# Expert inputs gathered from whole float32 rows, four one-time weight places, and transpositions moved between matrix products

## What is computed

```python
# t: 256 tokens x 1024; each token chooses 2 of the 8 experts of one group
combine = einsum('nk,nke->ne', top_w, one_hot(eid, 32))
for e in range(32):
    h = silu(t @ w_exp_gate[e]) * (t @ w_exp_up[e])
    y = y + combine[:, e:e + 1] * (h @ w_exp_down[e])
```

## Time and profile before

| | before |
|---|---|
| median of 3 runs | 1607.51 us (1607.12 to 1608.62) |
| the profiled execution's own time | 1607.49 us |
| its span | 1605.7 us |
| TensorE products busy | 1496.4 us (93%) |
| VectorE, ScalarE, GpSimd busy | 713.0, 574.6, 419.0 us |
| HBM read | 378.95 MB, mean 237 GB/s |
| mean granted TensorE clock | 0.984 of full speed |

### The profile page before, as it was taken

How to read it: one execution, slowest core, us unless ns; L and a number is a source line. 1 busy time by engine, 2 the same in 40 slices (tenths; PEclk the granted TensorE clock), 3 DMA queues, 4 the chain that set the end, 5 groups by cost and what they waited for, 6 DMA issues and landing times.

```text
span 1605.7 us, 23320 instructions
## 1 busy us (share of the span) xinstructions
PE 1496.4 (93%) x9442; PEld 1032.5 (64%) x9442; DVE 713.0 (44%) x1294; ACT 574.6 (36%) x779; POOL 419.0 (26%) x316
## 2 busy tenths in 40 slices
PE   5899999999999899999999998799989799999996
PEld 2788888888667444443344343477878678878785
DVE  2678887666436812111111121428222634334672
ACT  2432325554433322222121121344344355364662
POOL 0000000011000110000000000259867685757553
PEclk9999999999999999999999999999989899999998
DMA  8632225435778899999999999566436343434331
GB/s 310 204 127 96 79 79 173 139 107 165 265 264 295 360 378 420 421 422 422 422 422 422 422 422 422 204 231 210 132 130 222 110 166 106 158 111 151 106 134 64
DMA packets 120877, 381.10 MB, mean 237 GB/s; under 512 B 9302, under 2 KB 11134, under 8 KB 96222
## 3 DMA queue, kind: packets, MB, share of 16 engines
q1 hardware_dynamic: 120798, 380.02, 63.0%
HBM read 378.95 MB, written 1.05 MB: 237 GB/s over the span
## 4 chain that ended last, share of the span: by engine, by line
PE 67%; DMA 19%; DVE 4%; POOL 3%; ACT 3%; issue 2%; SPq 1%; POOLq 0%; DVEq 0%; ACTq 0%
DMA arena<-in_w_exp_up 17%; PE ps L786 12%; PE ps L793 12%; PE ps L787 12%; PE ps L1207 7%; POOL w_lo L2432 3%; PE ps L968 3%; PE ps L967 3%; PE ps L974 3%; PE ps L1219 2%; PE ps L867 2%; PE ps L887 1%; PE ps L1361 1%; ACT w_hi L2514 1%; PE ps L1230 1%
## 5 line engine op out<-in xcount | busy, mean ns | idle before, releaser
L2432 POOL TENSOR_TENSOR w_lo<-ring,w_hi 128x512 fp32r<-128x512 f32 x280 | 378.0, 1385 | 135.0 <-ACT w_hi L2514 123.3
L2514 ACT ACTIVATE w_hi<-ring 128x2048 fp32r<-128x2048 f32 x130 | 246.9, 1912 | 318.0 <-PE ps L793 148.6
L786 PE MATMUL ps<-w_hi,xt_hi 128*128 128x512 f32 x512 | 201.8, 394 | 0.2 <-ACT w_hi L2514 0.2
L787 PE MATMUL ps<-w_hi,xt_lo 128*128 128x512 f32 x480 | 187.0, 390 | 0.0
L1538 DVE TENSOR_TENSOR w_lo<-ring,w_hi 128x2048 fp32r<-128x2048 f32 x60 | 137.1, 2286 | 89.8 <-ACT w_hi L2514 89.4
L786 PE MATMUL ps<-w_hi,yt_hi 128*128 128x512 f32 x352 | 140.4, 399 | 5.5 <-DVE yt_lo L1531 2.7
L793 PE MATMUL ps<-w_lo,xt_hi 128*128 128x512 f32 x512 | 127.3, 391 | 5.1 <-POOL w_lo L2432 5.1
L1207 PE MATMUL ps<-arena 128*32 128x512 f32 x1056 | 118.9, 593 | 11.0 <-DMA arena<-in_w_exp_up 11.0
L2092 DVE TENSOR_SCALAR selT<-ps 128x256 fp32r<-128x256 f32 x32 | 13.6, 424 | 248.2 <-ACT arena L2845 248.2
L1207 PE MATMUL ps<-ring,arena 128*32 128x512 f32 x992 | 111.7, 593 | 12.0 <-DMA ring<-in_w_exp_up 11.0
L2432 POOL TENSOR_TENSOR w_lo<-ring,w_hi_ahead 128x512 fp32r<-128x512 f32 x8 | 9.9, 1271 | 422.6 <-ACT w_hi_ahead L2833 421.2
(11 more groups left out here) (323 smaller groups left out, 2378.1 us busy)
## 6 DMA issues: line engine op xcount, KB each, us to landing
ring<-in_w_in SPq DMA_DIRECT2D x40, 1024.0 KB, 5.1
ring<-in_b_w_in SPq DMA_DIRECT2D x40, 1024.0 KB, 5.1
arena<-in_w_exp_gate SPq DMA_DIRECT2D x33, 1024.0 KB, 23.0
arena<-in_w_exp_up SPq DMA_DIRECT2D x33, 1024.0 KB, 25.0
arena<-in_w_exp_down SPq DMA_DIRECT2D x32, 1024.0 KB, 23.3
ring<-in_w_exp_down SPq DMA_DIRECT2D x32, 1024.0 KB, 23.3
ring<-in_w_exp_gate SPq DMA_DIRECT2D x31, 1024.0 KB, 23.1
ring<-in_w_exp_up SPq DMA_DIRECT2D x31, 1024.0 KB, 25.0
```

Of the source, the lines that this page charges most:

```text
L786: pe.matmul(o[:, tt, :], hi[:, k, x_], w[:, c, :], start=(bias is None and j == 0 and c == 0), stop=False)
L787: pe.matmul(o[:, tt, :], lo[:, k, x_], w[:, c, :], start=False, stop=False)
L2432: ins = pool.tensor_tensor(w_lo2[:, slots_of[n], k, :], ring[:, slots_of[n], k, :], w[:, k, :].bitcast(F32), ALU.subtract)
L2514: act.activation(part_of(n)[1][:, :, :], ring[:, slots_of[n]], ACT.Copy).then_inc(S("w_hi_full"), 1)
```

## The change

- The bf16 parts go. `h_moe` is written to another place and stays as whole float32 rows, `sel` is float32, and `gather` does 2 products for a chunk, 16 for a pair. ScalarE's and VectorE's splitting instructions and the waits on `h_left` go.
- `extra` has four places (`EXTRA = 4`). The last two are filled after both router products (`routed`). The slots of expert 0's first four units are refilled with expert 4's units at once. The gains of the second norm are loaded after the third pair.
- Odd expert units 0, 1, 2 are asked for at `tail` 1,0, 1,1 and 2,0, units 4 and 5 at `tail` 6,0.
- `yT` is turned between tiles 9, 10, 11 and the first output units, `oT`'s first piece before the last value product, without `stay_busy`; ScalarE's and VectorE's shares move with them. The remainder of the first half of `bT` goes ahead of the second half's `normed_product`.

```diff
@@ places and order of SyncE
-        sel = nc.alloc_sbuf_tensor_at("sel", [P, NT, P], BF16, offset=ARENA_AT + 4 * (free0 + 4096))
+        sel, _ = carve(NT, P, on=free0 + 4096)
-        extra = [carve(UC, W, on=on)[0] for on in (o_S, o_S + 2048)]
+        extra = [carve(UC, W, on=on)[0] for on in (o_S + 2048, o_S, o_XT2, o_XT + 2048)]
-        h_parts = [nc.alloc_sbuf_tensor_at("h_part%d" % i, [P, NT, D], BF16, offset=ARENA_AT + 4 * (free0 + 1024 * i)) for i in range(3)]
-        h_rest, _ = carve(NT, D, on=o_XT + 2048)
-        h_moe, _ = carve(NT, D, on=o_qT)
+        h_moe, _ = carve(NT, D, on=free0)
...
-                if n in (at_unit["tail", 6, 0], at_unit["tail", 6, 1], at_unit["tail", 7, 0]):
-
-                    sp.wait_ge(S("unit_done"), end_of("ret", 1, 4))
-                    expert_unit(0, 1, n - at_unit["tail", 6, 0], 0)
-                if n == at_unit["tail", 7, 0]:
+                ahead = [at_unit["tail", 1, 0], at_unit["tail", 1, 1], at_unit["tail", 2, 0]]
+                if n in ahead:
+
+                    sp.wait_ge(S("retT_turned"), 4)
+                    expert_unit(0, 1, ahead.index(n), 0)
+                if n == at_unit["tail", 6, 0]:
...
+                sp.wait_ge(S("routed"), NT)
+                extra_unit(2)
+                extra_unit(3)
+                for k in range(6):
+                    sp.wait_ge(S("unit_done"), n_before + k + 1)
+                    expert_unit(4 if k < EXTRA else 2, 0, k, 0)
...
@@ TensorE
-                    for i, part in enumerate(h_parts):
-                        for tt in range(NT):
-                            mm = pe.matmul(ps[:, 0 if half else 2, o_:o_ + P], part[:, tt, P * k:P * (k + 1)], sel[:, tt, :],
-                                           start=(i == 0 and tt == 0), stop=(i == 2 and tt == NT - 1))
+                    for tt in range(NT):
+                        mm = pe.matmul(ps[:, 0 if half else 2, o_:o_ + P], h_moe[:, tt, P * k:P * (k + 1)], sel[:, tt, :],
+                                       start=(tt == 0), stop=(tt == NT - 1))
...
+            gemm_parts("a", 8, ("a", 8), xt2_hi, xt2_lo)
+            for t in range(9, 12):
+                gemm_parts("a", t, ("a", t), xt2_hi, xt2_lo)
+                turn_y(t - 9)
+            for j in range(4):
+                pair_evacuated(pe, ("yT", j))
+                gemm_unit("a_out", 0, j, yt_hi, yt_lo, 4)
+                if j == 0:
+                    turn_y(3)
+            gemm_parts("a_out", 1, ("a_out", 1), yt_hi, yt_lo, nk=4, half="y_half")
...
+                        if (g, c) == (2, 3):
+                            turn_output(0)
...
-                if c == 0:
-                    stay_busy(claim(("oT", c)), 12)
@@ VectorE
-            h_first_rest(0)
...
-            h_first_rest(1)
-            h_second_rest(0)
-            h_second_rest(1)
...
+                if t:
+                    rest_part("yT", t - 1, yt_hi, yt_lo)
+            rest_part("yT", 3, yt_hi, yt_lo)
...
                 product_scale(tt, 1, 4)
+                if tt:
+                    rest_tokens("bT", 0)
...
-            rest_tokens("bT", 0)
...
+                        if c == 3:
+                            rest_part("oT", 0, ot_hi, ot_lo)
                         join_last(c)
+                        if c == 2:
+                            gate_output(0)
...
-                if BKIND[t] == "z":
-                    gate_output(BIDX[t])
-            for c in range(2):
-                rest_part("oT", c, ot_hi, ot_lo)
+                if t == 19:
+                    gate_output(1)
+            rest_part("oT", 1, ot_hi, ot_lo)
@@ ScalarE
-            h_lead(0)
...
-            for tt in range(NT):
-                act.wait_ge(S("h_left"), tt + 1)
-                act.activation(h_parts[1][:, tt, :], h_rest[:, tt, :], ACT.Copy).then_inc(S("h_part"), 1)
...
-            for c in range(4):
-                lead_part("yT", c, yt_hi)
+                if t >= 9:
+                    lead_part("yT", t - 9, yt_hi)
+            lead_part("yT", 3, yt_hi)
...
-            leading_to(first["b_out"])
```

More of the change, by code:

```diff
@@ L53 @@
 PER_ROUND = 6 * NE
+EXTRA = 4
 RING2 = 4
@@ L260, in build @@
             slots_of.append(n % RING2 if n < n_before else expert_slot((n - n_before) // 6 % 2, (n - n_before) % 6) if n < first["a"] else (n - first["a"]) % RING2)
-            fills.append(slots_of.count(slots_of[n]))
+            fills.append(slots_of.count(slots_of[n]) - (n >= first["a"] and slots_of[n] in EVEN_SLOTS[:EXTRA]))
         fills_before = [slots_of[:n_before].count(k) for k in range(ALL_SLOTS)]
@@ L560, in weights @@
         def weights(odd, k, second=False):
-            if second and not odd and k < 2:
+            if second and not odd and k < EXTRA:
                 return extra[k]
@@ L1188, in arrived @@
                 s_ = expert_slot(odd, k)
-                if order == "second" and not odd and k < 2:
-                    pe.wait_ge(S("extra_full%d" % k), 16)
+                if order == "second" and not odd and k < EXTRA:
+                    pe.wait_ge(S("extra_full%d" % (k // 2)), 32)
                 else:
-                    missed = s_ in EVEN_SLOTS[:2] and order != "first"
+                    missed = s_ in EVEN_SLOTS[:EXTRA] and order != "first" and not (rd and s_ < RING2)
                     pe.wait_ge(full_of(s_, rd), e * 8 + 16 * (filled_times(s_, rd) + 1 - missed))
@@ L2228, in _ @@
                 dve.tensor_tensor(v, v, a_u[:, :, W * t:W * (t + 1)], ALU.mult).then_inc(S("y_gated"), 1)
-            for c in range(4):
-                rest_part("yT", c, yt_hi, yt_lo)
+                if t:
+                    rest_part("yT", t - 1, yt_hi, yt_lo)
+            rest_part("yT", 3, yt_hi, yt_lo)
             def part_sums(i, done):
```

44 lines of the change are left out of this document (12 added, 32 removed).

## The result

The changed kernel takes 1594.93 us (median of seven runs, 1589.88 to 1599.87); the kernel before, run beside it, 1608.62 us. The ratio is 0.9911 with a 95% interval of 0.9891 to 0.9931. The profiled execution is the one of 1594.93 us; its span is 1593.1 us, 12.6 us under the span of the kernel before (1605.7).

A forecast was written before the change was run, and what follows sets the result against it. Transfers were taken to bound the experts from 686 us, TensorE the rest, with three holes behind the experts. Gains of 7.5 (experts together) + 9.6 + 4.0 + 5.3 = 26.4 us gave 1581.1 us, range 1574 to 1591.

The forecast's parts named there:

- Part 1: Expert weight stream: two more one-time places leave two units less to carry after the stream resumes, 5.0 us gained.
- Part 2: First refills of expert slots: issued sooner, stream resumes 1.7 us earlier; 0.8 us more from a deeper queue.
- Part 3: Experts' input: float32 gather without split copies; first gate product 0.8 us earlier, pair about 1.0 us shorter but hidden.
- no saving: Rival on the experts' gather: 16 products take 3.5 us, pair 28.1 us, start 1.3 us later; 1582.5 us, 5%.
- The rival in which TensorE becomes the bound of all the experts: Expert loop: slow float32 gather makes a pair 31.6 us, total 1631 us; 4%.
- Part 4: Retention output stage: three early expert units delay its weights, TensorE 2.7 us later (0 to 7.5).
- Parts 5 to 7: Behind the experts: earlier yT turnings, bT remainder and oT turning gain 9.6, 4.0 and 5.3 us.
- No GpSimd remainder ends last: Rival on yT and oT: GpSimd's weight remainders end last, half of 14.9 us is lost; 1588.5 us, 9%.
- Prefetch dear, nothing earlier: Rival on early units: they cost 7.5 us, stream resumes no sooner; 1586 us, or 1590 with holes partly closed; 12%.

The follow-up runs named there:

- 3: The changed kernel with two one-time places instead of four, all else alike; 1593.49 us, ratio 0.9909.
- 1: The kernel before with only the moved yT and oT turnings and the earlier bT remainder; 1591.74 us, ratio 0.9888.
- 5: The kernel before with the moved turnings, earlier bT remainder and four one-time places, keeping its bfloat16 gather and its issue points for early expert units; 1587.71 us.
- kernel 2: The changed kernel with the five early expert units put back to where the kernel before issues them; 1588.09 us, ratio 0.9877.
- 10: The kernel before with only the yT turnings moved between the product tiles; 1599.90 us, ratio 0.9934.
- 11: The kernel before with only the earlier bT remainder and the moved oT turnings; 1599.93 us, ratio 0.9937.
- 6: As kernel 2, but three expert units issued earlier, in stretches where its transfers are idle; 1588.33 us, ratio 0.9868.
- second execution: The changed kernel measured once more with no edit; 1593.41 us, ratio 0.9898.
- kernel 7: As kernel 2, but the first early expert unit again issued ahead of the retention output stage's units; 1592.7 us.
- 8: As kernel 2, but the four one-time places hold units of expert 4 instead of expert 2, third pair written out ahead of the loops; 1591.43 us.

## Why the prediction went wrong, and where it was right

The spans differ by 12.6 us: 2.4 us lost ahead of 418 us, where the kernels are alike and 1.6 us are the clock's fall at 404 us; 6.6 lost in the stage; 0.7 between the stage and the first gate product; 2.7 gained in the experts; 19.7 gained behind them.

- *Part 1, two more places: 5.0 us forecast, about 0.5 measured (3).* This is the step that failed most. The working took the units in place as subtracted from a stream that then never stops. But the stream's lead over TensorE is bounded by the number of places, and a one-time place is one that does not come back: what it holds more at 555 us is missed in the hole at 596 us. The prediction looked for the hole ahead of the first refill only. With the bfloat16 gather, 1 and 5 differ by parts 1 and 2 together, and by 2.1 us in the experts, which is still far from the forecast.
- *Part 2, earlier resumption: 1.7 and 0.8 us forecast.* The first refill is indeed issued 3.66 us after the first gate product (568.79 for 565.13) and not 7.1; and in kernel 2, whose start is that of before, the window of 556 to 564 us has 401 GB/s where the earlier trace rows have 36. In after the start is so late that the places are full again: 176 GB/s from 564 to 572 us. Both together gave 1.5 us in the experts: 461.4 us is the mean of the four kernels with two places and the bfloat16 gather (before, 1, 10, 11), 459.9 that of the five with four places and the float32 gather. From the first gate product on, the sum had some 9.4 us.
- *Part 3, the gather: mis-sized by two.* The count behind the earlier trace rows was of instructions, not of products; the rows' x16 are eight products. At 256 columns 3.45 us for 8 are 0.43 us each, four cycles of 2.4 GHz for a column; at 128 columns it is a little more (0.24 us), and the Trainium skill (FP8 and Floating Point Precision, TensorE Precision Notes) was right with its four passes where the prediction said that the trace disagreed. The start of the experts is 0.7 us later instead of 0.8 earlier (103.3 us from the stage to it in before and 1, 104.0 in after, 2 and 6, all without a fall of the clock at 510 us). Between before and 2, the first gather and what follows up to the gate product take 4.97 us for 4.01, and TensorE's wait ahead of the second router product is 1.11 us for 1.56, so the forecast's 0.5 us for the copies was right and its 0.3 us for the gather was a loss of 1.0. In the loop, the pair grows from 27.4 to 28.3 us, as the rival "no saving" had it, and that moves the point from which the transfers bound the experts from 686 to 813 us. Yet by kernel 5 it costs the whole no more than the scatter. The rival in which TensorE becomes the bound of all the experts did not come.
- *Part 4, the early units: +2.7 us forecast, +6.6 measured, 4.8 in the second execution.* The first wait was right, 2.3 us for 2.1. For the second the forecast had 0.6 us; it was 2.6. Moved by the 2.4 us by which after is late there, the forecast has the unit landing at 437.0 us, and it landed at 439.0. The two transfers ahead of it landed where the forecast, moved so, has them (432.3 and 434.8 us by the issues' own times, forecast 432.1 and 434.5); this one came 4.2 us behind the early unit and not one transfer of 2.5 us. Two more were issued at 429.49 and 429.90 us, before it was in; that they took the rest of the rate is likely, but no run shows it. To this came the clock, 1.6 us in each of the four executions with three early units, which the prediction put at nothing. The upper bound of 7.5 us was named; it should have been nearer to the forecast.
- *Parts 5 to 7: 9.6, 4.0 and 5.3 us forecast; 10.3, 4.2 and 5.1 us in the trace of after* (by the chain's rows 1203.65 for 1206.93 us, 1271.46 for 1278.96, and the ends, each with the 7.1 us of the experts taken off). Kernels 1, 10 and 11 confirm the sum and that it adds up. No GpSimd remainder ends last in part 5; one of 6.0 us does behind part 6 in both kernels.
- *The rivals.* "Prefetch dear, nothing earlier" names what happened, at 1586 us; its stall of 7.5 us is near the 6.6 measured, but it still credited the two places with their 5.0 us and counted the gather as a saving. (The rival of no saving in the gather added 1.3 us where its own rows give 1.0; it decides nothing.) With the measured prices, 6.6 us for the stall, 0.7 for the gather at the start and 1.5 us back from parts 1 and 2, the forecast's own sum gives 1607.5+6.6+0.7-1.5-18.9 = 1594.4 us. That it meets the measured time so well is in part luck: the 2.4 us lost ahead of the stage are left out, and the experts of after were 1.2 us shorter than the 1.5 us make them.

## What to carry to other kernels

A store that is filled ahead pays only as far as it outlasts the slower side: count the places that come free while it is used up, and look for the hole where none does. Ahead of a stage whose weights are consumed as they land, every MB costs up to its transfer time, and with it perhaps a fall of the clock; and it buys nothing if the store is full at the time of its use anyway. And before a price is taken from a row, compare the row's number of instructions with the number of products that the code issues.

## What the runs showed of the hardware

- A product of float32 operands (not fp32r) appears as two TensorE rows, each 0.12 us at 128 moving columns: 0.24 us for a product (3.81 us for 16).
- A wait of 2 to 2.6 us of TensorE can bring its clock from the 2.4 to the 1.2 GHz level for eight products (0.43 us apart), or not: in after it fell behind the second wait (2.62 us) and not the first (2.32), in its second execution behind the first (2.23), and in kernel 7 a wait of 2.37 us was followed by products at full cadence.
- In some executions the clock also falls behind a wait of 2.16 us near 404 us that all kernels have (window 404 to 412 us: 0.79 in after, 1.00 before), and costs 1.6 us: the end of that wait's turning and the next group of remainder products are 7.7 us apart instead of 6.1. After has it and its second execution has not, so it belongs to no edit. The same holds behind the wait of 2.02 us near 510 us (window 508 to 516 us: 0.79 in 8, 1.00 in 2). A time of one execution can differ by 3 us through these two places alone.
